# One front stage for modulation, latents and mixing: scale folded into w_in, shift as a bias row, x turned once

## What is computed

```python
def branch_inputs(x, c, pos, ada_w, ada_b, norm_w, w_in, ...):
    mod = jnp.einsum('bd,de->be', jax.nn.silu(c), ada_w) + ada_b      # 1024 x 3072 weights
    shift, scale, gate = jnp.split(mod, 3, axis=-1)
    h = rmsnorm(x, norm_w) * (1 + scale[:, None, :]) + shift[:, None, :]
    z = jnp.einsum('btd,de->bte', h, w_in)                            # 1024 x 1952 weights
    q_lat = rmsnorm(z[..., OFF_Q:OFF_KV], q_norm_w)                   # 256 columns
    ckv = rmsnorm(z[..., OFF_KV:OFF_KR], kv_norm_w)                   # 128 columns
    kr = rope(z[..., OFF_KR:OFF_GA], pos)                             # 32 columns
    g_att = z[..., OFF_GA:OFF_U]; u = z[..., OFF_U:OFF_GP]; g_pool = z[..., OFF_GP:]   # 512 each
```

## Time and profile before

| | |
|---|---|
| median of 3 runs | 1558.01 us (1556.51 to 1560.98) |
| the profiled execution | 1564.0 us |
| its span, first to last instruction | 1562.3 us |
| mean granted PE clock | 0.955 of full |
| PE busy over the span | 1408.8 us, 90% |
| DVE, ACT, POOL busy | 776.2, 662.0, 539.0 us |
| attention's first instruction | 529.5 us after the start |

### The profile page before, as it was taken

The page is one execution under the profiler, slowest core; times in us unless marked ns, Lnnn a source line. Parts: engine busy times, 40 slices in busy tenths (PEclk is TensorE's granted clock), DMA queues, the critical chain, the costliest instruction groups (busy, mean ns, idle before and its releaser), DMA issues. The chain is left out here.

```text
span 1562.3 us, 23911 instructions
## 1 busy us (share of the span) xinstructions
PE 1408.8 (90%) x8312; PEld 1131.4 (72%) x8312; DVE 776.2 (50%) x1507; ACT 662.0 (42%) x1296; POOL 539.0 (34%) x458
## 2 busy tenths in 40 slices
PE   8788789999999679999999999999974899999987
PEld 1488779999999557777787777777752666666655
DVE  0587623233321386676767676667316244444443
ACT  0255422222221256666666666666753233333322
POOL 0355532322222423443434343433334433332210
PEclk9899989999999889999999999999985899999999
DMA  9243221121100200000000000000016765655420
GB/s 368 89 143 119 89 77 55 55 62 61 54 28 28 77 5 7 5 16 4 16 4 16 12 7 11 10 7 8 11 47 232 214 189 165 181 165 173 165 56 29
DMA packets 80692, 119.54 MB, mean 77 GB/s; under 512 B 17442, under 2 KB 63682, under 8 KB 78402
## 3 DMA queue, kind: packets, MB, share of 16 engines
q1 hardware_dynamic: 67980, 75.64, 16.8%
q0 software_dynamic: 3456, 27.26, 4.7%
q10 hardware_dynamic: 9168, 15.50, 2.8%
HBM read 95.73 MB, written 22.90 MB: 76 GB/s over the span
## 5 line engine op out<-in xcount | busy, mean ns | idle before, releaser
L1181 POOL TENSOR_TENSOR pt_lo<-pt,pt_hi 128x512 fp32r<-128x512 f32 (+2 forms) x160 | 171.5, 1072 | 257.4 <-ACT pt_hi L1086 257.1
L1085 ACT ACTIVATE pt<-att_ps_s 128x512 f32<-128x512 f32 (+1 forms) x320 | 170.4, 533 | 145.5 <-PE att_ps_s L1340 80.8
L1241 DVE TENSOR_REDUCE mx<-att_ps_p 128x1 f32<-128x512 f32 (+2 forms) x300 | 177.4, 607 | 96.9 <-PE att_ps_p L1310 76.5
L1252 DVE TENSOR_TENSOR pt_lo<-pt,pt_hi 128x512 fp32r<-128x512 f32 (+1 forms) x160 | 122.4, 765 | 94.8 <-ACT pt_hi L1086 93.5
L1086 ACT ACTIVATE pt_hi<-att_ps_s 128x512 fp32r<-128x512 f32 (+1 forms) x320 | 169.2, 529 | 0.0
L108 PE MATMUL mix_ps_u<-mix_h_hi,wb_hi 128*128 128x256 f32 x512 | 146.2, 285 | 0.0
L110 PE MATMUL mix_ps_u<-mix_h_hi,wb_lo 128*128 128x256 f32 x512 | 144.8, 283 | 0.0
L109 PE MATMUL mix_ps_u<-mix_h_lo,wb_hi 128*128 128x256 f32 x512 | 144.8, 283 | 0.0
L108 PE MATMUL out_ps_y<-wo_hi,mixed_hi 128*128 128x512 f32 x272 | 125.2, 460 | 12.2 <-POOL mixed_lo L1963 11.6
L108 PE MATMUL att_ps_o<-pt_hi,v_hi 128*128 128x512 f32 (+1 forms) x320 | 127.0, 397 | 9.8 <-DVE pt_lo L1252 8.5
L1338 PE MATMUL att_ps_s<-q_hi,k_hi 97*128 97x512 f32 (+1 forms) x320 | 119.0, 372 | 1.6 <-issue 1.6
(11 more groups left out here) (339 smaller groups left out, 3201.6 us busy)
## 6 DMA issues: line engine op xcount, KB each, us to landing
ada<-in_ada_w_dram SPq DMA_DIRECT2D x8, 1536.0 KB, 16.6
lat_x<-in_x_prompt_dram SPq DMA_DIRECT2D x16, 512.0 KB, 3.9
mix_x<-in_x_prompt_dram SPq DMA_DIRECT2D x16, 512.0 KB, 3.7
x_rows<-in_x_prompt_dram SPq DMA_DIRECT2D x16, 512.0 KB
out_dram<-y ACTq DMA_DIRECT2D x16, 512.0 KB, 7.4
lat_wraw<-in_w_in_dram POOLq DMA_DIRECT2D x8, 768.0 KB
gate_att_scratch<-gate_a SPq DMA_DIRECT2D x16, 256.0 KB, 2.3
pool_scratch<-mixed SPq DMA_DIRECT2D x32, 128.0 KB, 2.1
```

Of the source, the lines that this page charges most:

```text
L1085: act.activation(pt[:, k % 2, 0:n], ps_s[:, k % 2, 0:n], ACT.Exp, scale=SCALE)
L1181: pool.tensor_tensor(ph[1][:, k % 4, 0:n], pt[:, k % 2, 0:n], ph[0][:, k % 4, 0:n].bitcast(F32), ALU.subtract).then_inc(p_lo_ready[1], 1)
L1241: dve.tensor_reduce(mx[:, I % 2, r, c:c + 1], chunk_bank(g, n)[:, 0:width], AX.X, ALU.max).then_inc(chunk_read, 1)
L1252: dve.tensor_tensor(ph[1][:, k % 4, 0:n], pt[:, k % 2, 0:n], ph[0][:, k % 4, 0:n].bitcast(F32), ALU.subtract).then_inc(p_lo_ready[0], 1)
```

## The change

The first three stages become one. Its parts:

- Only the 2048 shift and scale columns of `ada_w` are loaded first, in eight chunks of 1 MB, each with a place of its own. Four matmuls for each chunk write to four strips of 32 partitions of one PSUM bank (`c_act` is padded to 32 columns), so that one DVE addition adds the bias and four transposes turn the result.
- The 1024 gate columns are loaded by POOL's queue and multiplied inside the first step, two chunks behind each of its four groups, into two strips of the bank `ps_y`; they go to `gate_d`.
- `w_in` comes in eight whole rows of chunks (1952 columns, 1 MB) through a ring of three slots. ACT scales by `coef_a` as it rounds to the high part, DVE multiplies by `coef_a` and subtracts for the low part.
- The shift is no longer added to h. The ninth column of `hs` holds it; its product with the raw `w_in` is a row of biases, computed together with the samples' z in plain float32, in four strips. It goes to `zs_d` and is read back as `bw_rows` (added to each latent row) and as `bw_turn`, which PE turns to `bw_cols` (the bias operand of ACT's evictions).
- x is loaded, squared, scaled (by ACT) and turned once for each block. ACT reads the high part of h out of PSUM, DVE subtracts for the low part out of PSUM; `h_values` is gone. `ps_x` has one buffer of two banks, `ps_z` one bank, `ps_u` three, `ps_y` one.
- A step now is: latent rows of block 0, group 0, latent rows of block 1, group 1, `turn_lat`, `turn_x`, group 2, `mix`, `turn_lat`, `turn_x`, group 3, `mix`, two pairs of gate columns, two more `mix`.
- Square roots and Silu now alternate on ACT within a step.
- The turned latents go to device memory (`lat_d`) by a third transfer for each block on ACT's queue, and attention loads them in four chunks of 768 KB behind its first weights and `kr`.

```diff
+            def load_w(c):
+                if c >= NR:
+                    sp.wait_ge(w_lo_ready, c - NR + 1)
+                    sp.wait_ge(samples_done, c - NR + 1)
+                sp.dma_start(raw[c % NR][:], w_in[:, c, :]).then_inc(raw_in[c % NR], 16)
...
+            for k in range(KC):
+                sp.dma_start(ada[:, k, :], ada_rows[:, k, 0:2 * D]).then_inc(ada_in[k], 16)
+                if k == 1:
...
+            for b in range(2):
+                load_x(b, b)
+            for c in range(KC):
+                load_w(c)
...
+            sp.wait_ge(zs_ready, 1)
+            for g in range(4):
+                cols = COLS[g]
+                sp.dma_start(zs_d[:, cols], zs[g * STRIP:g * STRIP + NC, 0:cols.stop - cols.start]).then_inc(zs_out, 16)
+            sp.wait_ge(zs_out, 64)
+            sp.dma_start(bw_rows[:], zs_d[DB, 0:LA].partition_broadcast(P)).then_inc(bw_in, 16)
+            sp.dma_start(bw_turn[:], zs_d[DB, LA:].rearrange("(t p) -> t p", p=P)).then_inc(bw_in, 16)
...
+            def w_high(c):
+                act.wait_ge(raw_in[c % NR], 16 * (c // NR + 1))
+                act.activation(w[0][:, c, :], raw[c % NR][:], ACT.Copy, scale=coef_a[:, c, DB:NC]).then_inc(w_hi_ready, 1)
...
             def body(s, e):
                 for b in range(2):
+                    squares(s, 2 * s + b, b)
+                    root(2 * s + b, b)
+                    keep_u(s, b)
+                for b in range(2):
+                    keep_lat(2 * s + b, b)
                     if exists(s + 1, NS):
                         h_high(s + 1, 1 - e, b)
-                    keep_u(s, 2 * b)
-                    keep_u(s, 2 * b + 1)
+                    keep_u(s, 2 + b)
...
-            def h_values(n):
-                dve.wait_ge(x_turned, n + 1)
-                if exists(n - 1, NB):
-                    dve.wait_ge(h_lo, n)
-                for c in range(KC):
-                    last = dve.tensor_scalar(h32[:, c * P:(c + 1) * P], ps_x[:, c // 4, (c % 4) * P:(c % 4 + 1) * P],
-                                             coef_a[:, c, DB:NC], coef_b[:, c, DB:NC], ALU.mult, ALU.add)
-                last.then_inc(h_ready, 1)
...
+            def h_low(s, e, b):
+                cols = slice(b * P, (b + 1) * P)
+                dve.wait_ge(h_hi, 2 * s + b + 1)
+                dve.tensor_tensor(hb[e][1][:, :, cols], ps_x[:].rearrange("p a (c s) -> p (a c) s", s=P),
+                                  hb[e][0][:, :, cols].bitcast(F32), ALU.subtract).then_inc(h_lo, 1)
+
+            def w_low(c):
+                dve.wait_ge(w_hi_ready, c + 1)
+                dve.scalar_tensor_tensor(out=w[1][:, c, :], in0=raw[c % NR][:], scalar=coef_a[:, c, DB:NC],
+                                         in1=w[0][:, c, :].bitcast(F32), op0=ALU.mult, op1=ALU.subtract).then_inc(w_lo_ready, 1)
...
+            for c in range(KC):
+                if c == KC - 1:
+                    dve.wait_ge(samples_done, KC)
+                    wide = COLS[3].stop - COLS[3].start
+                    dve.tensor_copy(zs[0:3 * STRIP, :], ps_zs[0:3 * STRIP, :])
+                    dve.tensor_copy(zs[3 * STRIP:, 0:wide], ps_zs[3 * STRIP:, 0:wide]).then_inc(zs_ready, 1)
+                w_low(c)
+                if c < 2:
+                    h_low(0, 0, c)
...
+                for b in range(2):
+                    rows(s, e, b)
+                    if first and b == 0:
+                        pe.wait_ge(bw_in, 32)
+                        pe.transpose(ps_l[:, 0:12], bw_turn[:], ident[0:12, 0:12]).then_inc(bw_turned, 1)
+                    group(b)
+                for b in range(2):
+                    if first and b == 0:
+                        pe.wait_ge(bw_ready, 1)
+                    turn_lat(2 * s + b, b)
                     if exists(s + 1, NS):
                         turn_x(2 * s + 2 + b, b)
-                    group(s, e, 2 * b)
-                    group(s, e, 2 * b + 1)
...
+                    group(2 + b)
+                    if not first:
+                        mix(s, b)
...
+            for k in range(KC):
+                pe.wait_ge(ada_in[k], 16)
+                for g in range(4):
+                    last = pe.matmul(ps_mod[g * STRIP:(g + 1) * STRIP, :], c_act[:, k, :], ada[:, k, g * 512:(g + 1) * 512],
+                                     start=(k == 0), stop=(k == KC - 1), skip_group_check=True)
...
+            for c in range(NGRP):
+                cols = slice(c * 512, (c + 1) * 512)
+                sp.dma_start(lat_t[:, :, cols], lat_cols[:, :, cols]).then_inc(lat_in[c], 16)
+                if c == 0:
+                    sp.dma_start(rope[:], t["c_rope_cols"]).then_inc(rope_in, 16)
+                    sp.dma_start(wv_raw[:], t["w_uv"].rearrange("a k h d -> (a k) (h d)")).then_inc(wv_in, 16)
...
             for c in range(NGRP):
+                act.wait_ge(lat_in[c], 16)
                 act.activation(lat_hi[:, :, c * 512:(c + 1) * 512], lat_t[:, :, c * 512:(c + 1) * 512],
                                ACT.Copy).then_inc(lat_hi_ready, 1)
```

More of the change, by code:

```diff
@@ new lines, in build @@
+        y_done, y_step, mixed_ready = sem("y_done"), sem("y_step"), sem("mixed_ready")
+        mixed_out = [sem(f"mixed_out{g}") for g in range(NG)]
+        a_out = [sem("a_out0"), sem("a_out1")]
+        bw_turned, bw_ready = sem("bw_turned"), sem("bw_ready")
+        prev_done, prev_ready, prev_out = sem("prev_done"), sem("prev_ready"), sem("prev_out")
+        HALF = NS // 2
+        LEVELS = sum(g + 1 for g in range(NG))
+        ada_rows = t["ada_w"].rearrange("a (c p) n -> p (a c) n", p=P)
@@ L716, in _ @@
             for b in range(2):
-                h_high(0, 0, b)
+                square_x(2 + b, b)
+            for b in range(2):
+                x_rms(2 + b, b)
             for b in range(2):
@@ new lines, in body @@
+                if exists(s + 1, NS):
+                    h_low(s + 1, 1 - e, 0)
+                if isinstance(s, int) and s == 0:
+                    h_low(s + 1, 1 - e, 1)
+                    dve.wait_ge(gate_used, KC)
+                    dve.tensor_tensor(gate_b[:], gate_b[:], ps_y[0:2 * STRIP, :], ALU.add).then_inc(gate_kept, 1)
+                mix(s, 0)
+                pooled_values(s, 2, 6)
+                if exists(s + 1, NS) and not (isinstance(s, int) and s == 0):
+                    h_low(s + 1, 1 - e, 1)
@@ new lines, in _ @@
+            dve.wait_ge(bias_in, 96)
+            dve.wait_ge(mod_summed, 1)
+            dve.tensor_tensor(mod[:], ps_mod, bias[:], ALU.add).then_inc(mod_ready, 1)
+            for b in range(2):
+                x_variance(b, b)
+            dve.wait_ge(mod_turned, 1)
+            dve.wait_ge(vec_ready, 1)
+            turned = ps_turned.rearrange("p (q r) -> p q r", q=GRP)
+            for g in range(2):
+                dve.tensor_copy(coef_b[:, g * GRP:(g + 1) * GRP, :], turned[:, :, g * STRIP:g * STRIP + NC])
@@ new lines, in _ @@
+            for g in range(2):
+                last = dve.scalar_tensor_tensor(
+                    out=coef_a[:, g * GRP:(g + 1) * GRP, :], in0=turned[:, :, (2 + g) * STRIP:(2 + g) * STRIP + NC], scalar=1.0,
+                    in1=vec_t[:, g * GRP:(g + 1) * GRP].unsqueeze(2).broadcast_to([P, GRP, NC]), op0=ALU.add, op1=ALU.mult)
+            last.then_inc(coef_ready, 1)
+            for b in range(2):
+                x_rstd(b, b)
+            dve.wait_ge(coef_ready, 1)
+            dve.wait_ge(xs_turned, 1)
@@ new lines, in mix, with group @@
+                if g >= 1 or exists(s - 1, NS):
+                    pe.wait_ge(y_step, 4 * s + g)
+                pe.matmul(ps_y[:, 0:T], w_pool[:, g, :], pooled[:, g % 2, :], start=True, stop=True).then_inc(y_done, 1)
+            def body(s, e):
+                first = isinstance(s, int) and s == 0
+                def group(g):
+                    columns(s, e, g, (OFF_U + g * P, OFF_GP + g * P))
+                    if first:
+                        for k in range(2 * g, 2 * g + 2):
+                            gates(k)
+                for b in range(2):
+                    rows(s, e, b)
[3 more added lines that the diff above has]
+                    group(b)
+                for b in range(2):
+                    if first and b == 0:
+                        pe.wait_ge(bw_ready, 1)
+                    turn_lat(2 * s + b, b)
@@ L890, in _ @@
-            samples(2)
-            pe.wait_ge(zs_ready, 3)
+                    group(2 + b)
+                    if not first:
+                        mix(s, b)
+                if first:
+                    mix(s, 0)
+                columns(s, e, 4, (0, P))
+                if first:
+                    mix(s, 1)
+                columns(s, e, 5, (2 * P, 3 * P), (0,))
+                mix(s, 2)
+                columns(s, e, 5, (2 * P, 3 * P), (1,))
+                mix(s, 3)
+            pe.wait_ge(const_in, 16)
@@ L892, in _ @@
+            pe.wait_ge(mod_ready, 1)
+            for q in range(GRP):
```

(8 more changed lines are left out.)

943 lines of the change are left out of this document (383 added, 560 removed).

## The result

The changed kernel takes 1497.4 us (median of 4 runs, 1494.3 to 1502.3), the kernel before 1558.6 (4 runs, 1556.5 to 1561.0): a ratio of 0.961, 95% interval 0.9585 to 0.9635. Measured a second time (five runs) it was 0.9627 (0.9599 to 0.9655). The forecast was 1492 with a range of 1474 to 1518. The profiled execution took 1497.2 us, its span 1495.4 against 1562.3.

The account below looks back on a forecast made before the run. PE was taken as the bound, fully in the mixing stage. The stage ends 71.3 us earlier, the reload adds 5: -66.3, from 1564.0 to 1498, less 6.0 for the median: 1492, range 1474 to 1518 with rivals.

Parts of the forecast that it names:

- The step: Steady mixing step, all PE: 38.0 us plus two latents blocks without x turning, 47.9, and 0.4 for switches between work.
- The tightest place: In a step, the second x turn waits for DVE's h_low to free ps_x; margin 1.5 us, so no PE wait.
- slower than before: Rival, chance 0.03: POOL's windows stretch DVE's h_low; needs 9.4 us of PE wait in a step.
- The drain and the table loads: ACT in a step: six loads of 1.28 us hidden behind PE; the skill's 1.38 us drain per switch not counted.
- The start of the body: End of the prelude: PE waits for the bias row until 63.0 us, 64.7 with the low clock.
- the low clock: After idling for the bias row PE starts at a lower clock: 1.7 us added before the body.
- The ring's cycle of 9.2: Prelude, w_in's three-slot ring: a slot takes 5.1 landing, 1.9 ACT and 2.2 DVE, 9.2 us in all.
- The way of the bias row: Prelude: z in SBUF at 57.0, stores 1.7 issue and 2.1 landing, loads 2.2; PE waits 3.5 us, until 63.0.
- The strips: Modulation, samples and gates: four column strips overlap on PE, so an ada_w chunk costs 1.0 instead of 5.1 us.
- the 1516 of the rival: Rival, chance 0.06: strips do not overlap; modulation 10 later, samples about 8, gates 6 more, giving 1516 us.
- The end of the stage: Merged stage ends at 455.6 us instead of 526.9, 71.3 less: 64.7 + 386.6 - 4.6 + 8.9.
- The reload: Attention's start: loading turned latents delays the kr_cols copy 6 us; 5 taken as cost, from 3.3 to 8.

Follow-up runs that it names:

- e3_turn_twice: Changed kernel with every x block turned twice in a row, eight more transposes per block: 1524.1 us, ratio 0.9766 to the kernel before.
- e5_late_high: Changed kernel with ACT writing the high part of h four times instead of once from the second step on: 1508.3 us, ratio 0.9662.
- e4_no_tables: Changed kernel with the step loop's three square roots replaced by copies, removing six ACT table loads a step: 1501.7 us, ratio 0.9625.
- e2_tables_late: Changed kernel with the six small tables issued behind the last chunk of w_in instead of the fourth: 1500.8 us, ratio 0.962.
- e8_both: Changed kernel with w_in chunks landing in place, tables behind the last chunk, and attention's first latent chunk ahead of its weights: 1490.1 us, ratio 0.9558.
- e11_gates_last: e8_both plus z read out by ACT, its stores split between SP and ACT, gate columns loaded behind the bias row: 1489.7 us, ratio 0.9546.
- e12_both_again: e8_both measured again with nothing edited: 1489.6 us, ratio 0.9565.
- e6_in_place: Changed kernel with every w_in chunk given a place of its own, so SP waits for no ring slot: 1495.6 us, ratio 0.9604.
- e7_latents_first: Changed kernel with attention's first latent chunk issued ahead of its weights and the rope table last: 1498.7 us, ratio 0.9627.

## Why the prediction was right, and where its steps were off

The mechanism and the sum held: the forecast was 66.3 us less by the profiled execution, and the spans differ by 66.9. That they agree within 0.6 us is luck: the start of the body came 3.7 us later than forecast, the body was 6.2 shorter, attention began 1.5 later behind it, and the reload cost 0.4 more.

- **The step** was priced at 47.9 from rows and 0.4 for the changes between kinds of work. It takes 47.48, and e3_turn_twice confirms that nothing hides a transpose, at about its row's price (0.11 against 0.10); the other kinds of work were not varied. The 0.4, chosen inside 0 to 1.0, was not there at all. From the first group to the end of the stage this makes 384.7 us instead of 390.9 (386.6 - 4.6 + 8.9): 6.2 too much.
- **The tightest place** was right: margin 1.5 forecast, 1.6 in the trace, 1.5 to 2.1 by e5_late_high, and both its ends were right too: `h_low` ends 26.8 us into the step (26.9) and PE turns x at 28.4 (28.4). `h_low` takes 1.22 us in each of the 16 blocks, so POOL's windows never stretched it, as the rival "slower than before" would have needed. The drain and the table loads were rightly left out (e4_no_tables).
- **The start of the body** was forecast at 63.0, 64.7 with the low clock counted; it is 68.4. The coefficients were ready at 30.8 instead of 28.7, as the modulation's last product ended at 27.7 and not at 25.5. The low part of chunk 1 ended at 40.4 instead of 39.4. The ring's cycle of 9.2 was right from chunk 4 on (9.0). The miss is in the first turn of the ring: chunk 4 was given 5.1 us from the freed slot to its landing and took 9.5 from its issue at 40.77, behind six tables. The tables were overlooked: they are in the queue that the prediction followed, and without them in front (e2_tables_late) 4.7 us pass, close to the 5.1, and the last low part starts 2.9 earlier. The way of the bias row was sized at 6.0 and took 5.6. PE's wait for it was not 3.5 but 0.8, since its latent rows did not end 0.3 behind the last low part but 2.5 behind it, at 67.4: they began at 61.1, behind the last product of the samples' z, and the first nine of their matmuls were about 0.35 apart instead of 0.19. So a low clock was met, but under the wait. As an addition the 1.7 was met in e2_tables_late (7.4 instead of 5.9: 1.5), e5_late_high and e8_both, and not in the changed kernel, e11_gates_last or e12_both_again.
- **The strips** overlap as the earlier trace rows had it; without that the kernel would be at the 1516 of the rival.
- **The end of the stage**: the stage ends at 453.1 (455.6 forecast), 73.8 us earlier, but 4.1 us instead of 2.6 pass until attention starts; so it starts 72.3 us earlier, with 71.3 forecast for the end of the stage.
- **The reload** was sized at 5, between 3.3 and 8. The copy of `kr_cols` came 8.0 late, not 6: ACT split the first latent chunk 8.1 us after attention's start, not 7.1, and the last at 17.5, not 15.6, since it waited for every one of the four and for the weights between them (6.8 and 1.8 us in the lines above). PE's lower clock there (0.74 against 0.82) was not in the sum. At the first product of probabilities and values it is 7.0; over everything behind attention's start it is 1038.2 - 1032.8 = 5.4, inside the variation named above.
- **From the profile to the median.** The forecast took 6.0 off, the distance of the profiled execution before (1564.0) from its median. By the profiled execution the forecast was 1498, and 1497.2 was measured; but the profiled execution after lies at its own median (1497.4). The medians differ by 61.2, not 66.3: the 5.4 us between forecast and result are this term. The record says where the 6 us come from: the profiled execution before had a mean granted clock of 0.955, lower than any of the 32 other executions of that kernel whose clock is on record (0.958 to 0.964), and the time goes with the clock (1559.4 to 1563.5 us at 0.958, 1554.3 to 1556.7 at 0.964). So the 6 us belonged to that execution and not to the kernel. They do not seem to lie in the later stages: from the first product of probabilities and values to the end it has 967.4 us, and the thirteen profiles of the changed kernel and its variants have 965.4 to 971.8 (median 967.5). Then most of them lie ahead of that mark, and the 72.3 and 7.0 us read there from this pair of profiles carry them: together they are 65.3, where the medians have 61.2. With a single profile of the kernel before, that split is argued and not shown.

The prediction warned of a wait inside the step before anything else. None came, and nothing is lost there until the chain is 1.6 us longer.

## What to carry to other kernels

When a stretch is bound by TensorE and everything else in it has a margin, price it by adding distances between starts from the trace, and add nothing for switching between kinds of work unless a row shows it. Ahead of such a stretch follow each issuing queue entry by entry, small tables too: what is in flight or in front decides when the next chunk lands, and a small store whose data PE wants back waits behind bulk loads that nobody needs yet. Do not carry the distance of one profiled execution from its median over to the changed kernel, and look at its granted clock beside those of the other executions first; here that step alone made the whole distance between forecast and result.

## What the runs showed of the hardware

- The issue of a transfer on SP can itself be held: 10.45 us for a 32 KB table in e6_in_place, and 7.8 us for the same table in e8_both, where such a table takes 0.5 in the changed kernel (40.17 to 40.67). Taking out the waits of the program does not issue transfers earlier than this allows.
- After a wait of 3.03 us (e2_tables_late) PE's next matmuls ran partly at half clock, the first group in 7.4 us instead of 5.9. In e12_both_again a wait of 2.85 us at the same place left it at the full clock (1.00 over the first group), but in e5_late_high the first group was slow (7.3 us) behind a wait of only 1.6 us. The length of the wait alone does not tell; what PE did before it may count, and that was not tried.
- A branch back in the instruction loop left PE idle for 4.75 us once, in the kernel whose loop was longer by 32 transposes a pass (e3_turn_twice), and not in the changed kernel. Instructions were being transferred during the stall (16 KB at 273.2 us) and not at all around the changed kernel's branch (254 to 360 us). An edit that only adds cheap instructions can cost this beside them.
- The same kernel is slower in executions with a lower mean granted clock: e4_no_tables took 1491.6 us at 0.961 and 1507.2 at 0.950, e7_latents_first 1496.1 at 0.959 and 1504.6 at 0.951.
